# Idle products on TensorE in the waits of a decoder trunk's first norm

## The reference

```
c_act = silu(c)
for i in range(DEPTH):                       # DEPTH = 2
    mod = (c_act @ ada_w[i] + ada_b[i])[:, None, :]
    sh1, sc1, g1, sh2, sc2, g2 = jnp.split(mod, 6, axis=-1)
    h = rms_norm(x, norm_mix_g[i]) * (1 + sc1) + sh1
    y = gla_mixer(h, ...) if i % 2 == 0 else moba_mixer(h, ...)
    x = x + g1 * y
    h = rms_norm(x, norm_mlp_g[i]) * (1 + sc2) + sh2
    x = x + g2 * (jnp.square(jax.nn.relu(h @ mlp_w1[i])) @ mlp_w2[i])
```

## Time and profile before

| | |
|---|---|
| three executions, us | 643.11, 643.47, 643.63 |
| span of the profiled execution, us | 642.6 |
| around the span, against the median, us | 0.9 |
| PE busy | 617.6 us, 96% of the span |
| DVE, ACT, POOL busy | 474.3, 341.8, 39.5 us |
| bytes moved | 156.43 MB, mean 243 GB/s |

### The profile page before, as it was taken

How to read it: one execution, slowest core, us unless ns; L and a number is a source line. 1 busy time by engine, 2 the same in 40 slices (tenths; PEclk the granted TensorE clock), 3 DMA queues, 4 the chain that set the end, 5 groups by cost and what they waited for, 6 DMA issues and landing times.

```text
span 642.6 us, 9093 instructions
## 1 busy us (share of the span) xinstructions
PE 617.6 (96%) x3391; PEld 515.0 (80%) x3391; DVE 474.3 (74%) x660; ACT 341.8 (53%) x581; POOL 39.5 (6%) x65
## 2 busy tenths in 40 slices
PE   3699999999999999999999999999999999999997
PEld 2367875677889989998977788788789899899985
DVE  4638998898778978889897898766786555455455
ACT  3437632658654354445458688666954453444440
POOL 3030011000000101010100000000000000000000
PEclk9699999999999999999999999999999999999999
DMA  8999599678488998999982665344476555556501
GB/s 287 387 356 395 180 318 384 224 247 277 156 284 316 376 366 306 351 363 337 360 320 82 246 197 196 133 126 155 132 267 225 171 182 188 191 196 196 196 0 65
DMA packets 59084, 156.43 MB, mean 243 GB/s; under 512 B 2818, under 2 KB 3312, under 8 KB 59056
## 3 DMA queue, kind: packets, MB, share of 16 engines
q1 hardware_dynamic: 47296, 112.41, 49.9%
q0 software_dynamic: 11760, 43.67, 19.2%
HBM read 155.02 MB, written 1.05 MB: 243 GB/s over the span
## 4 chain that ended last, share of the span: by engine, by line
PE 82%; DVE 10%; DMA 3%; issue 2%; ACT 2%; SPq 0%; DVEq 0%; ACTq 0%
PE ps L503 14%; PE ps L504 14%; PE ps L505 14%; PE ps L700 7%; PE ps L699 7%; PE ps L698 7%; PE ps L510 4%; PE ps L511 3%; PE ps L512 3%; DMA arena<-in_ada_w_dram 3%; DVE w_lo L1433 1%; DVE spare L1433 1%; DVE ada_acc L1450 1%; PE ps L607 1%; PE ps L622 1%
## 5 line engine op out<-in xcount | busy, mean ns | idle before, releaser
L1051 ACT ACTIVATE w_hi<-w_raw 128x1024 fp32r<-128x1024 f32 x180 | 189.2, 1058 | 205.0 <-PE ps L505 107.0
L1433 DVE TENSOR_TENSOR w_lo<-w_raw,w_hi 128x1024 fp32r<-128x1024 f32 x180 | 217.9, 1222 | 94.5 <-ACT w_hi L1051 94.3
L699 PE MATMUL ps<-a_lo,w_hi 128*128 128x256 f32 x384 | 108.7, 283 | 0.0
L700 PE MATMUL ps<-a_hi,w_lo 128*128 128x256 f32 x384 | 108.7, 283 | 0.0
L698 PE MATMUL ps<-a_hi,w_hi 128*128 128x256 f32 x384 | 108.6, 283 | 0.0
L503 PE MATMUL ps<-w_hi,m_hi 128*128 128x512 f32 x256 | 100.4, 392 | 0.0
L504 PE MATMUL ps<-w_lo,m_hi 128*128 128x512 f32 x256 | 99.8, 390 | 0.0
L505 PE MATMUL ps<-w_hi,m_lo 128*128 128x512 f32 x256 | 99.7, 389 | 0.0
L503 PE MATMUL ps<-w_hi,a_hi 128*128 128x512 f32 x224 | 92.7, 414 | 5.1 <-DVE a_lo L1587 5.1
L504 PE MATMUL ps<-w_lo,a_hi 128*128 128x512 f32 x224 | 88.3, 394 | 0.0
L505 PE MATMUL ps<-w_hi,a_lo 128*128 128x512 f32 x224 | 88.3, 394 | 0.0
(11 more groups left out here) (202 smaller groups left out, 708.9 us busy)
## 6 DMA issues: line engine op xcount, KB each, us to landing
w_raw<-in_mlp_w_dram SPq DMA_DIRECT2D x64, 1024.0 KB, 5.5
ada_raw<-in_ada_w_dram POOLq DMA_DIRECT2D x40, 1024.0 KB, 6.7
w_raw<-in_gla_w_in_dram SPq DMA_DIRECT2D x12, 1024.0 KB, 14.7
w_raw<-in_moba_w_in_dram SPq DMA_DIRECT2D x12, 1024.0 KB, 7.3
ada_raw<-in_ada_w_dram SPq DMA_DIRECT2D x4, 1024.0 KB, 13.2
arena<-in_ada_w_dram SPq DMA_DIRECT2D x4, 1024.0 KB, 14.3
w_raw<-in_gla_w_out_dram SPq DMA_DIRECT2D x4, 1024.0 KB, 9.3
w_raw<-in_moba_w_out_dram SPq DMA_DIRECT2D x4, 1024.0 KB, 5.0
```

The lines of the kernel that those rows point to most:

```text
L699: mm(o, w_hi[:, u, w], a_lo[:, a, :], start=False, stop=False)
L700: z = mm(o, w_lo[:, u, w], a_hi[:, a, :], start=False, stop=u == 3 and k == 1)
L1051: A(dst, w_raw[:, c // 2, c % 2], ACT.Copy).then_inc(hi_made, 1)
L1433: V.tensor_tensor(out, w_raw[:, c // 2, c % 2], w.bitcast(F32), ALU.subtract).then_inc(lo_made, 1)
```

## The change

A helper `awake(n, bank)` issues `n` f32 products of the 128x128 identity with itself into the first 128 columns of a PSUM bank. Nothing reads those results. The helper is called six times in `first_norm` on PE: 9 products before the turns, 10 between the two halves of block 0, 5 after the turn of the small vectors, 3 before the second half of block 2, 2 before its `ada_cols`, and 11 behind it, before u0. A wait for `set_up`, which DVE's first memsets raise, now stands also at the head of the function. Other engines' programs are the same.

```
+            def awake(n, bank):
+
+                for _ in range(n):
+                    mm(ps[:, bank, 0:P], eye[:, :], eye[:, :], start=True, stop=True)
+
             def first_norm():
+                pe.wait_ge(set_up, 3)
+                awake(9, 7)
                 for tb in range(TB):
                     turn_norm(0, tb)
                 pe.wait_ge(c_ok, 1)
                 pe.wait_ge(pos_ok, 1)
                 tr(ps[:, 4, KC:KC + TB], pos_f[:, :], eye[0:TB, 0:TB]).then_inc(pos_T, 1)
                 pe.wait_ge(set_up, 3)
-                for half in range(2):
-                    ada_rows(0, half, 6)
+                ada_rows(0, 0, 6)
+                awake(10, 7)
+                ada_rows(0, 1, 6)
                 pe.wait_ge(vec_in, 16 * N_VEC)
                 tr(ps[:, 5, 0:N_ROWS], rows[0:N_ROWS, :], eye[0:N_ROWS, 0:N_ROWS]).then_inc(vec_T, 1)
+                awake(5, 7)
                 ada_rows(2, 0, 7)
                 pe.wait_ge(pos_cp, 1)
                 ada_cols(0, 4)
+                awake(3, 6)
                 ada_rows(2, 1, 7)
                 pe.wait_ge(vec_ok, 1)
+                awake(2, 6)
                 ada_cols(1, 5)
+                awake(11, 6)
```

## The result

| | before | after |
|---|---|---|
| median of 22 executions, us | 643.13 | 644.38 |
| lowest, highest | 641.08, 645.16 | 642.67, 645.80 |
| span of the profiled execution, us | 642.6 | 641.8 |
| granted clock, mean of that execution | 0.988 | 1.000 |

The ratio of the times is 1.0016, with a 95% interval of 1.0009 to 1.0024. The kernel became slower by 1.0 us (0.6 to 1.5). Yet the profiled execution is 0.8 us shorter than that of before. Both facts have to be explained, and neither trace alone is a typical execution: the profiled one of after took 643.55 us (1.75 us around its span of 641.8). With as much around it, the one of before, at 642.6, would have been a slow 644.4.

The account below looks back on a forecast made before the run. PE bounds, at half clock from 19.8 to 33.2 us, with the gate chain on ACT and DVE bounding at 85.57. PE's -3.1 is absorbed whole; 642.6 + 0.6 = 643.2, with 0.9 around it 644.1 us; range 641.4 to 645.7.

Parts of the forecast that it names:

- Cost of the products: In PE's waits before u0: 0.49 us each at half clock, nine 4.4 us, all hidden in waits, taken as 0.
- Gain on PE: Block 2's second half and u0 on PE run at full clock: 4.3 us gained together.
- The first date that doesn't move: Block 1's second half lands at 31.34 us, so PE waits until 31.4 and its shift is 3.1 us.
- POOL's steps earlier: POOL's steps 0 and 1, released by PE's rows of block 3, go out 3.1 us earlier, at 37.4.
- m3: SP's transfer for ACT's u6 lands at about 49.1 us instead of 44.05; u6 begins 1.1 us later than before.
- Equal shares: Rival on the DMA queues: SP's gets 0.2 MB/us, m3 lands at 45.8, m5 bounds; -1.8 us, 641.7; 20%.
- the slide: POOL's traffic moved 3.1 us earlier as a whole; SP's queue then gets 1.44 MB to 42.9, 0.55 to 48.9.
- The gate: GLA's gate chain on ACT and DVE, from 58.86 us before, starts late by +0.6 us, L1621 at 59.4.
- the absorption: PE's 3.1 us lead is lost whole in waits by the update at 85.57 us, which comes at 86.2.
- The end: Profiled span 642.6 + 0.6 = 643.2; with the 0.9 us that the median has around it, 644.1 us.
- the clock falls again: Rival: half clock in new PE waits of 71 to 86 us; 13.4 us of it cost 6.7, about 649; 6%.
- the prediction's own sign of being wrong: m3 at or before 46 with L1621 before 58, or a clock of 0.50 anywhere between 13 us and the end.

## Why the prediction was right, and where not

The forecast was 644.1 us, the measurement 644.38. By step:

- *Cost of the products*: right. 0.25 us each at full clock (2.70 us for eleven) and nothing on the path; u0 waits 0.76 us behind them. The nine took 3.76 us, 0.42 each, less than the 4.4 allowed. That the first two groups are needed was not claimed, and they are not.
- *Gain on PE*: right. The clock is full, u0 starts at 26.10 (predicted about 26.5).
- *The first date that doesn't move*: right. L607 waits 1.13 us for block 1's second half and starts at 31.20 (predicted 31.4); the lead is 3.2 us (3.1).
- *POOL's steps earlier*: right, 37.28 (37.4).
- *m3*: mechanism right, size wrong. It landed at 46.25, not at 49.1. Sliding POOL's traffic as a whole was too hard on SP's queue: the queue moved 1.37 MB from 37 to 43 and 0.80 from 43 to 49, not 0.55. Equal shares, by which m3 would have come at 45.8, were nearer than the slide. What I did not name was m4. It came 3.1 us late and set the gate: ACT's u8 waited 4.19 us for it. A part of what was priced at m3 is therefore found at m4. The DMA queues of after over 37 to 43 us (SP's), and over 43 to 49 (POOL's, then SP's; packets, MB, share), and last those of before over 50 to 52:

```profile
q1 hardware_dynamic: 691, 1.37, 78.5%
...
q0 software_dynamic: 406, 1.60, 67.6%
q1 hardware_dynamic: 402, 0.80, 35.1%
...
q0 software_dynamic: 186, 0.72, 90.7%
q1 hardware_dynamic: 49, 0.09, 13.0%
```

  The packets settle what the prediction left open. With both large loads under way the queues moved equal numbers of packets, 406 and 402, but POOL's hold 3.9 KB and SP's 2.0 KB. The have the same sizes (1.84 MB in 474, 0.55 in 284). Their 0.55 MB is the mean of two stretches, though: 288 packets to 235 from 46 to 50 us, then 186 to 49. The slide took that mean as the rate behind m3. By equal packets, from the 0.94 MB that SP's queue moved from 43 to 50, the 0.57 MB missing at 42.9 take 4.2 us and m3 lands at 47.1, an estimate; it was 46.25. Why SP's queue fell back from 50 to 52 in the kernel before is open.

- *The gate*: mis-sized, and with the wrong sign. +0.6 was the term; the trace shows -0.5. Against the traced execution of before the absorption was 2.6 of 3.2 us, not 3.7.
- *The end*: the 0.9 us around the span was wrong for the traced execution of before; 1.75 us is what the executions of after show. With that, the sum would have given 643.2 + 1.75 = 645.0 for a slow start, and a typical one lies lower. Errors cancelled in part: the traced before was slow (its clock of 0.988 does not explain that, as executions of 0.988 have a median of 643.2), the gate came earlier and not later, and half of the executions of after lose clock.
- *The rival "the clock falls again"* was given 6%. A lower clock was seen in 18 of 34 executions, at 1.4 us and not 6.7; whether in the waits that the rival named is not shown. A mean of 0.997 over 643 us comes to some 4 us at 0.50, an estimate, where the rival took 13.4. Without it (the 16 others, 643.53) the change is near nothing: 0.1 to 0.4 us above the medians of before, 643.13 to 643.40. So by these medians most of the added time goes with the lower clock; the absorption explains why PE's 3.2 us bring nothing against it. By the prediction's own sign of being wrong (a clock of 0.50 anywhere after 13 us) those executions fail it, though neither trace does.

The chances named the right outcome for a reason that is right in its main part: PE's lead is absorbed, because POOL's earlier steps delay SP's pieces. That the sum came within 0.3 us is luck. Its gate term had the wrong sign, and the loss that goes with the lower clock, which it did not hold, made up for that.

The Trainium skill ("DMA: Bandwidth & Descriptors", Queues, rings and completion order) has engines take turns between queues, a packet at a time. The trace of after agrees, with 406 packets to 402, as far as the profile's packets are the ones meant.

## What to carry to other kernels

Work that arrives earlier also releases its transfers earlier. Before pricing a gain at the start, list what the faster engine triggers and what is still in the DMA queues then; here 2 MB that went out 3 us earlier cost the lead. Products that compute nothing are a fair tool against a falling clock, but each wait at which the clock falls has to be filled where it is, and the gain itself can create new ones later. When executions differ by more than the effect, sort them by mean clock before comparing traces, for one trace is one of several starts.

## What the runs showed of the hardware

- Products of the identity with itself in PE's waits held the clock: 1.00 from 19.8 to 33.2 us where there had been 0.50, with two to eleven of them in each wait.
- A single wait can make the clock fall. Ahead of the same projection, 1.77 us went with a lower clock in 2 of 12 executions, 2.64 us in 11 of 12, and, filled, in 1 of 11; a wait of 3.7 us ahead of u0 in 9 of 10. Waits of 1.7 us ahead of the update went with 14 of 22, 4 of 12, 4 of 12 and 1 of 12, in four groups of executions, so one such wait does not decide it.
- At the start of an execution the granted clock can read 1.00 where the durations say otherwise: eight turns took 1.94 us without the nine products and 1.10 with them, both at 1.00 in the profile.
- When POOL's large transfers joined a full queue of SP's, SP's share fell to 0.80 of 2.40 MB in six us, with equal numbers of packets (402 and 406) of 2.0 and 3.9 KB; in the kernel before to 0.55 of 2.39, with 284 packets against 474.
